# Router logits taken per chunk in five accumulator banks, and expert positions by ten products

## Chip, cores and metric

One NeuronCore of one Trainium2 chip runs the whole program in one launch. The metric is the device time of one execution in microseconds (us). Engines are TensorE (PE for products, PEld for its weight loads), VectorE (DVE), ScalarE (ACT), GpSimd (POOL) and SyncE (SP, which here issues most DMAs).

## What is computed

One step of a two-layer backbone on 640 tokens (128 context, 512 latent; width 1024). The change lies in the second layer's expert network:

```python
def moe_ffn(h, router_w, w_gu, w_down):
    x = h.reshape(B * L, D)
    probs = jax.nn.softmax((x @ router_w).astype(f32), axis=-1)
    top_p, top_i = lax.top_k(probs, TOP_K)                  # 2 of 8
    top_p = top_p / jnp.sum(top_p, axis=-1, keepdims=True)
    gates = jnp.einsum('nk,nke->ne', top_p, jax.nn.one_hot(top_i, N_EXPERTS, dtype=f32))
    for e in range(N_EXPERTS):
        y = y + gates[:, e:e + 1] * swiglu(x, w_gu[e], w_down[e]).astype(f32)
```

`h` is the normed and modulated trunk: `rmsnorm(x, w) * (1 + scale) + shift`.

## The kernel before

The engines run their own instruction lists and meet at semaphores. Activations stand transposed: `hT` holds 8 chunks (`KD`) of 128 features, each 640 tokens wide, that is `NT` = 5 tiles of 128 tokens.

**Accumulators.** `ps` has four slots of 1024 f32 columns, two banks of 512 each. `Ring(4)` deals them out: step j of a stage uses slot j % 4, and `R.plan` counts the uses stage by stage. TensorE calls `take` (wait until the slot's former use is freed), sets `ps_full` with its last product, the reader waits with `full` and frees with `ps_free`; `done` waits for that.

**Weights.** SP loads weight blocks of up to 1 MB into a ring of five places (`load`, L459), in the order of `loads`; a place is loaded again when the step named in the last field of its entry is full. The router's weights (32 KB, 8 chunks of 8 columns) are one such block, "rt". The experts' blocks follow, and need the expert's number first, which DVE writes to `item_expert` (semaphore `items_ready`).

**norm3** (L687 to L730). ACT squares xT, TensorE sums the squares with a matrix of ones (L717), ACT makes `rstd`, DVE writes `hT` chunk by chunk (L728), and ACT adds the shift in place, chunk by chunk (L708), raising `h_ready` by one per chunk: 32 when norm3's last chunk is there.

**Router, TensorE** (`pe_router`). It waits for `h_ready` 32. For each token tile t it sums over the eight chunks k the product of hT's 128 x 128 block (the weights of the array) with the router's 8 columns, 40 products into columns t*8 of one slot. Then 40 transposes turn hT to rows of tokens, eight per tile, each tile in a slot ("ht", L1895). Then the positions ("cnt"): for each tile t, the sum over u < t of `ones` times the one-hot rows of tile u, and the triangle `tri[0]` times those of tile t, so that each token has its rank within its expert; 15 products, and 5 more for the counts.

**Router, DVE** (`dve_router`). It copies the logits (L1912), takes the two largest of each token and their indices (L1915 to L1919), makes the one-hot rows `oh` (L1924 to L1926), the weights (L1928 to L1930), then the low part of each transposed tile, `hlo` (L1934, after ACT's high part `hhi`, L2120). It copies positions and counts (L1937, L1938) and works out the number of items, their experts, and each token's place; `items_ready` comes at L1961, `sel` (L1973, L1976) and `slot_i` (L1968) behind it. POOL adds hhi and hlo to rows (L2178) and scatters these by `slot_i` (L2185).

**Experts.** TensorE gathers the first item's tokens by products with `sel` (`pe_gather`), then runs a loop over items (up to 256 token rows of one expert each), the count and the expert being read from `item_expert` at run time. ACT makes the high part of each weight block (L1996), DVE and POOL the low part (L2002). `rows` of an item are stored and gathered back at the end.

All products go through `mm` (L580). An f32 product shows as two records, each with its load. The other norms use the same helpers; `pe_first`, behind norm2, has a loop with the chunk outermost:

```python
for k in range(KD):
    nc.tensor.wait_ge(h_ready, h_base + k + 1)
    for c in range(chunks_):
        ...
```

Of the kernel before, what the change touches and what calls it, by code (L numbers as in the profile page):

```python
# [29 lines left out]
P = 128  # L30
D = 1024
KD = D // P
# [12 lines left out]
NE = 8  # L45
# [99 lines left out]
def program(nc, I, O):  # L145
    with ExitStack() as ctx:
# [205 lines left out]
        for stage, each, turns in (  # L352
                ("lam", 2, 1), ("mod", 4, MOD_FIRST // 2), ("norm0", 1, 1), ("qkv", 12, 1), ("z", 4, 1), ("gat", 1, 1),
                ("qk", 16, 1), ("l2", 8, 1), ("vb", NT, 1), ("att0", len(plan_b), 1), ("obn", H, 1),
                ("cum", 1, 1), ("tri", len(TRI), 1), ("scan", len(STEP), 1), ("omod", len(OMOD), 1), ("onrm", NT, 1), ("eo", 4, 2),
                ("norm1", 1, 1), ("fgu", 2 * FC, 1), ("fdn", 2, 4),
                ("norm2", 1, 1), ("oi", 7, 1), ("mlan", 2, 1), ("uqn", HC, 1), ("uqr", 8, 1), ("kn", HC, 1),
                ("vv", NT + 1, 1), ("att1", len(plan_c), 1), ("oo", 4, 2),
                ("norm3", 1, 1), ("rt", 1, 1), ("ht", NT, 1), ("cnt", 1, 1), ("moe0", 4, 1),
                ("moe", len(ITEM), ITEMS)):  # L360
            R.plan(stage, each, turns)

# [18 lines left out]
        def take(stage, j, turn=0):  # L381
            s, n, _, free = slot_use(stage, j, turn)
            if not (isinstance(n, int) and n == 0):
                nc.tensor.wait_ge(free[s], n)
            return s

        def full(eng, stage, j, turn=0):
            s, n, written, _ = slot_use(stage, j, turn)
            eng.wait_ge(written[s], n + 1)
            return s  # L390

        def done(eng, stage, j, turn=0):
            s, n, _, free = slot_use(stage, j, turn)
            eng.wait_ge(free[s], n + 1)
# [18 lines left out]
            "kn": (I["w_ukv"][0:1], WB, 1, 1, lambda j: ("kn", HC - 1)),  # L413
            "vv": (I["w_ukv"][1:2], WB, 1, 1, lambda j: ("vv", NT)),
            "oo": (I["w_oo"], WB, 2, 2, lambda j: ("oo", 2 * j + 1)),
            "rt": (I["w_rt"], 64, 1, 1, lambda j: ("rt", 0)),
            "moe": (None, WB, EC + 6, ITEMS, None),
        }
        order = [(stage, j, turn) for stage, (_, _, each, turns, _) in loads.items() if stage != "moe"
# [13 lines left out]
        def block(stage, j, turn=0):  # L433
            s, n = wuse(stage, j, turn)
            nc.tensor.wait_ge(w_full[s], 16 * (n + 1))
            return wring[:, s, :]
# [142 lines left out]
        def mm(out, lhsT, rhs, first, last):  # L579
            return nc.tensor.matmul(out, lhsT, rhs, start=first, stop=last)  # L580
# [1300 lines left out]
        bigf = tmp[:, MISC + 960:MISC + 960 + ITEMS + 1]  # L1881
        whof = tmp[:, MISC + 800:MISC + 800 + ITEMS + 1]

        def pe_router():
            nc.tensor.wait_ge(h_ready, 32)
            w, s = block("rt", 0), take("rt", 0)
            for t in range(NT):
                for k in range(KD):
                    last = mm(ps[:, s, t * NE:(t + 1) * NE], hT[:, k, t * P:(t + 1) * P], w[:, k * NE:(k + 1) * NE],
                              k == 0, k == KD - 1)  # L1890
            last.then_inc(ps_full[s], 1)
            for t in range(NT):
                s = take("ht", t)
                for k in range(KD):
                    last = nc.tensor.transpose(ps[:, s, k * P:(k + 1) * P], hT[:, k, t * P:(t + 1) * P], ident)  # L1895
                last.then_inc(ps_full[s], 1)

            nc.tensor.wait_ge(oh_ready, 1)
            s = take("cnt", 0)
            for t in range(NT):  # L1900
                for u in range(t + 1):
                    mm(ps[:, s, t * NE:(t + 1) * NE], tri[0] if u == t else ones, oh[:, u, :], u == 0, u == t)
            for u in range(NT):
                last = mm(ps[:, s, NT * NE:(NT + 1) * NE], ones, oh[:, u, :], u == 0, u == NT - 1)
            last.then_inc(ps_full[s], 1)

        def dve_router(dve, st):


            dve.wait_ge(mla_out, 32)  # L1910
            s = full(dve, "rt", 0)
            nc.vector.tensor_copy(gates_sb[:, 0:NT * NE], ps[:, s, 0:NT * NE]).then_inc(ps_free[s], 1)  # L1912
            done(dve, "rt", 0)
            for t in range(NT):
                last = nc.vector.max(top[:, t, :], rt[:, t, :])  # L1915
            st.then(last)
            for t in range(NT):
                st.then(nc.vector.max_index(topi[:, t, :], top[:, t, :], rt[:, t, :]))
            nc.vector.tensor_copy(topf, topi)  # L1919
            nc.vector.tensor_tensor(tw, top[:, :, 1], top[:, :, 0], ALU.subtract).then_inc(top_ready, 1)  # L1920
            dve.wait_ge(top_ready, 1)
            for t in range(NT):
                for i, o in enumerate((oh1, oh2)):
                    last = nc.vector.tensor_scalar(o[:, t, :], iota[:, 0:NE], topf[:, t, i:i + 1], None, ALU.is_equal)  # L1924
            st.then(last)
            nc.vector.tensor_tensor(oh, oh1, oh2, ALU.add).then_inc(oh_ready, 1)  # L1926
            dve.wait_ge(top_exp, 1)
            st.then(nc.vector.tensor_scalar(tokw[:, 1, :], tw, 1.0, None, ALU.add))  # L1928
            st.then(nc.vector.reciprocal(tokw[:, 0, :], tokw[:, 1, :]))
            st.then(nc.vector.tensor_tensor(tokw[:, 1, :], tw, tokw[:, 0, :], ALU.mult))  # L1930
            for t in range(NT):
                dve.wait_ge(hhi_ready, t + 1)
                s, _ = R.use("ht", t)
                nc.vector.tensor_tensor(hlo[:, t, :], ps[:, s, :], hhi[:, t, :].bitcast(F32), ALU.subtract  # L1934
                                        ).then_inc(ps_free[s], 1)
            s = full(dve, "cnt", 0)
            nc.vector.tensor_copy(pos, ps[:, s, 0:NT * NE].rearrange("p (t e) -> p t e", e=NE))  # L1937
            nc.vector.tensor_copy(cnt, ps[:, s, NT * NE:(NT + 1) * NE]).then_inc(ps_free[s], 1)  # L1938
            done(dve, "cnt", 0)

            st.then(nc.vector.tensor_scalar(tiles_e, cnt, 0.0, None, ALU.is_gt))
            for m in range(1, -(-T // IT)):
                st.then(nc.vector.scalar_tensor_tensor(tiles_e, cnt, float(m * IT), tiles_e, ALU.is_gt, ALU.add))
            st.then(nc.vector.tensor_tensor_scan(last_e, ones[:, 0:NE], tiles_e, 0.0, ALU.mult, ALU.add))
            nc.vector.tensor_tensor(cmp, spread(last_e, 1, ITEMS + 1), spread(iota[:, 0:ITEMS + 1], 2, NE), ALU.is_le)
            nc.vector.tensor_tensor(started, last_e, tiles_e, ALU.subtract)
            st.then(nc.vector.tensor_tensor(first_e, last_e, tiles_e, ALU.subtract))
            nc.vector.tensor_reduce(whof, cmp, AX.X, ALU.add)
            st.then(nc.vector.tensor_scalar(first_e, first_e, float(IT), -1.0, ALU.mult, ALU.add))
            st.then(nc.vector.tensor_scalar(whof, whof, float(NE - 1), None, ALU.min))  # L1950
            nc.vector.tensor_copy(item_expert[0:1, 0:ITEMS + 1], whof[0:1, :])
            nc.vector.tensor_copy(item_expert[0:1, ITEMS + 1:ITEMS + 2], last_e[0:1, NE - 1:NE])

            st.then(nc.vector.scalar_tensor_tensor(endp, first_e, 1.0, cnt, ALU.add, ALU.add))
            st.then(nc.vector.scalar_tensor_tensor(cmp, spread(iota[:, 0:ITEMS + 1], 2, NE), float(-IT),
                                                   spread(endp, 1, ITEMS + 1), ALU.mult, ALU.add))
            nc.vector.tensor_tensor(begun, spread(iota[:, 0:ITEMS + 1], 2, NE), spread(started, 1, ITEMS + 1), ALU.is_ge)
            st.then(nc.vector.tensor_scalar(cmp, cmp, float(P), None, ALU.is_gt))
            st.then(nc.vector.tensor_tensor(cmp, cmp, begun, ALU.mult))
            st.then(nc.vector.tensor_reduce(bigf, cmp, AX.X, ALU.add))  # L1960
            nc.vector.tensor_copy(item_expert[0:1, ITEMS + 2:2 * ITEMS + 3], bigf[0:1, :]).then_inc(items_ready, 1)  # L1961

            st.then(nc.vector.tensor_tensor(pos, pos, spread(first_e, 1, NT), ALU.add))
            for i, o in enumerate((oh1, oh2)):
                st.then(nc.vector.tensor_tensor(prd, pos, o, ALU.mult))
                st.then(nc.vector.tensor_reduce(slot_of[:, i, :], prd, AX.X, ALU.add))
            dve_select(st)
            nc.vector.tensor_copy(slot_i[:, :, :], slot_of[:, :, :]).then_inc(slot_ready, 1)  # L1968
# [628 lines left out]
```

## Time and profile before

| | us |
|---|---|
| median of 3 runs | 2578.08 |
| lowest, highest | 2575.83, 2585.19 |
| profiled execution, whole time | 2584.36 |
| its span | 2581.9 |
| mean granted TensorE clock of it | 0.926 |

| engine | busy us | share |
|---|---|---|
| PE | 2305.9 | 89% |
| PEld | 2017.9 | 78% |
| DVE | 1057.6 | 41% |
| ACT | 888.7 | 34% |
| POOL | 479.7 | 19% |

Times in the views count from the start of the span. "L580" is line 580 of the kernel; a line can be that of a helper. In a timeline a row is a run of like instructions on one engine, with the idle time before it and what ended that in brackets. "PEclk" is the clock that TensorE was granted, 1.00 being 2.4 GHz and 0.50 being 1.2 GHz.

### The profile page before, as it was taken

The page shows a single profiled execution, that of the slowest core. Times are in us where ns is not written, and L with a number is a line of the kernel's source. Part 1 is how long each engine was busy: PE and PEld are TensorE (multiplying, and loading weights), DVE is VectorE, ACT ScalarE, POOL GpSimd, SP SyncE. Part 2 cuts the span into 40 slices and gives each one's busy share as a digit, 9 for nine tenths or more (in the row PEclk, how much of TensorE's full clock was granted, in tenths as well). Part 3 has the DMA queues.
Part 4 walks back from the last instruction along what each step waited for, and adds up shares of the span by engine and source line. Part 5 has one row for each costly group of instructions (what it writes and reads, how often), then busy time and mean ns, then how long its engine had stood idle before and what let it go on. Part 6 is the DMA issues. An engine that isn't in the chain of part 4 may idle for free.

```text
span 2581.9 us, 35367 instructions
## 1 busy us (share of the span) xinstructions
PE 2305.9 (89%) x14334; PEld 2017.9 (78%) x14335; DVE 1057.6 (41%) x1537; ACT 888.7 (34%) x1259; POOL 479.7 (19%) x266
## 2 busy tenths in 40 slices
PE   6999887848898999989998999969998899998994
PEld 4896665538767999989965587968898888897893
DVE  2521264445723222232113455232335777744534
ACT  3321244212114111131032134124345666644444
POOL 0100002463002000020000000024223454523321
PEclk8989987759999999989999899969999999999997
DMA  6121003940431222211210000017547878866655
GB/s 286 51 90 49 33 25 132 336 176 11 170 114 49 82 69 80 67 45 68 84 56 19 1 33 34 1 49 274 176 172 273 324 307 330 344 227 236 247 190 170
DMA packets 70078, 353.68 MB, mean 137 GB/s; under 512 B 12112, under 2 KB 17872, under 8 KB 37296
## 3 DMA queue, kind: packets, MB, share of 16 engines
q1 hardware_dynamic: 65200, 337.28, 35.5%
q0 software_dynamic: 4736, 14.26, 1.5%
q8 instruction: 119, 1.95, 0.3%
q14 instruction: 23, 0.19, 0.0%
HBM read 318.06 MB, written 33.46 MB: 136 GB/s over the span
## 4 chain that ended last, share of the span: by engine, by line
PE 62%; issue 15%; POOL 9%; DVE 7%; ACT 4%; DMA 3%; SPq 0%; POOLq 0%; DVEq 0%; ACTq 0%
PE ps L580 58%; POOL wring_x L2002 6%; PE ps L717 1%; PE ps L984 1%; ACT arena L1036 1%; POOL tmp L1202 1%; DVE tmp L1487 1%; POOL tmp L1200 1%; POOL arena_x L1689 1%; DVE tmp L1427 1%; DMA xT<-in_x 1%; DVE att L1006 1%; DMA wring<-in_w_mod 1%; POOL rows L2185 0%; ACT hT L708 0%
## 5 line engine op out<-in xcount | busy, mean ns | idle before, releaser
L580 PE MATMUL ps<-arena_x,hT_x 128*128 128x256 f32 (+1 forms) x2536 | 355.8, 293 | 34.3 <-issue 34.3
L580 PE MATMUL ps<-arena_x 128*128 128x320 f32 (+3 forms) x1698 | 361.5, 352 | 17.0 <-DVE arena_x L1976 8.9
L2002 POOL TENSOR_TENSOR wring_x<-wring,arena_x 128x2048 fp32r<-128x2048 f32 (+1 forms) x60 | 284.2, 4745 | 459.1 <-ACT arena_x L1996 459.0
L580 PEld LDWEIGHTS ps<-arena_x,hT_x 128*128 128x128 f32 x2536 | 329.0, 199 | 38.6 <-issue 36.6
L580 PEld LDWEIGHTS ps<-arena_x 128*128 128x128 f32 (+1 forms) x1698 | 279.2, 192 | 65.5 <-issue 31.6
L1996 ACT ACTIVATE arena_x<-wring 128x2048 fp32r<-128x2048 f32 x153 | 284.2, 1857 | 100.4 <-DMA wring<-in_w_mgu 100.4
L2002 DVE TENSOR_TENSOR wring_x<-wring,arena_x 128x2048 fp32r<-128x2048 f32 (+1 forms) x90 | 215.3, 2401 | 81.3 <-ACT arena_x L1996 81.3
L580 PE MATMUL ps<-hT,wring 128*128 128x320 f32 x832 | 233.4, 443 | 12.1 <-ACT hT L708 10.6
L580 PEld LDWEIGHTS ps<-hT,wring 128*128 128x128 f32 x832 | 162.1, 195 | 83.6 <-issue 20.2
L580 PE MATMUL ps<-tmp_x,arena_x 128*128 128x320 f32 x1024 | 165.9, 314 | 6.0 <-ACT hT L708 6.0
L580 PEld LDWEIGHTS ps<-tmp_x,arena_x 128*128 128x128 f32 x1024 | 156.7, 192 | 6.7 <-issue 6.5
L580 PE MATMUL ps<-tmp_x,wring_x 128*128 128x320 f32 x1024 | 161.3, 309 | 0.0
L580 PE MATMUL ps<-wring_x,hT_x 128*128 128x256 f32 x1120 | 153.2, 286 | 8.1 <-POOL wring_x L2002 7.9
L580 PE MATMUL ps<-hT_x,arena_x 128*128 128x320 f32 x960 | 152.8, 310 | 1.2 <-DVE arena_x L1061 0.7
L580 PEld LDWEIGHTS ps<-tmp_x,wring_x 128*128 128x128 f32 x1024 | 152.9, 188 | 0.1
L580 PEld LDWEIGHTS ps<-wring_x,hT_x 128*128 128x128 f32 x1120 | 142.9, 194 | 10.0 <-POOL wring_x L2002 9.1
L580 PEld LDWEIGHTS ps<-hT_x,arena_x 128*128 128x128 f32 x960 | 144.2, 189 | 1.7 <-DVE arena_x L1061 0.9
L2135 ACT ACTIVATE expf<-ps 128x256 f32<-128x256 f32 x110 | 42.2, 384 | 229.0 <-PE ps L580 228.9
L1583 DVE SCALAR_TENSOR_TENSOR xT<-ps,modcol,xT 128x128 f32<-128x128 f32 (+2 forms) x72 | 27.2, 434 | 209.1 <-PE ps L580 209.1
L2225 DVE TENSOR_TENSOR expf<-expf,ps 128x256 f32<-128x256 f32 x110 | 45.4, 415 | 158.7 <-ACT expf L2135 158.7
L1744 DVE TENSOR_TENSOR arena<-arena,ps 128x640 f32<-128x640 f32 x22 | 18.1, 821 | 213.3 <-PE ps L580 213.3
L691 ACT ACTIVATE tmp<-xT 128x640 f32<-128x640 f32 x32 | 22.0, 730 | 180.0 <-DVE xT L1583 154.9
(305 smaller groups left out, 3188.9 us busy)
## 6 DMA issues: line engine op xcount, KB each, us to landing
wring<-in_w_mgu SPq DMA_DIRECT2D x105, 1024.0 KB, 6.0
wring<-in_w_mod SPq DMA_DIRECT2D x48, 1024.0 KB, 9.5
wring<-in_w_mdn SPq DMA_DIRECT2D x30, 1024.0 KB, 5.6
wring<-in_w_gu SPq DMA_DIRECT2D x22, 1024.0 KB, 4.8
wring<-in_w_mdn SPq DMA_DIRECT2D x20, 768.0 KB, 5.2
wring<-in_w_ev SPq DMA_DIRECT2D x14, 1024.0 KB, 5.0
rows<-hT SPq DMA_DIRECT2D x1, 12288.0 KB, 34.5
wring<-in_w_dn SPq DMA_DIRECT2D x16, 704.0 KB, 4.1
```

The source lines that it names most:

```text
L580: return nc.tensor.matmul(out, lhsT, rhs, start=first, stop=last)
L717: last = nc.tensor.matmul(pair(s)[:, half, :], ones, tc[:, k, half * HT:(half + 1) * HT], start=(k == 0), stop=(k == KD - 1))
L984: last = nc.tensor.transpose(ps[:, s, n * P:(n + 1) * P], probs(i, 0)[:, n * P:(n + 1) * P], ident)
L1006: nc.vector.tensor_reduce(cells(i)[:, st_:st_ + 1], src, AX.X if t == 0 else AX.XY, ALU.max, negate=True).then_inc(mx_ready, 1)
L1036: nc.scalar.activation(dst, src, ACT.Exp, bias=cells(i)[:, st_:st_ + 1], accum_out=cells(i)[:, 2 + st_:3 + st_]).then_inc(ps_free[s], 1)
L1200: st.then(eng.tensor_tensor(part, L[:, k + 1:B32, k:k + 1].broadcast_to([NB, rest, n]), X[:, k:k + 1, 0:n].broadcast_to([NB, rest, n]), AL ...
L1202: last = eng.tensor_tensor(X[:, k + 1:B32, 0:n], X[:, k + 1:B32, 0:n], part, ALU.subtract)
L1583: last = nc.vector.scalar_tensor_tensor(xs, ps[:, s, at:at + b - a], modcol[:, bass.ds(c * 2 + (gate * 16 + grp), 1)], xs, ALU.mult, ALU.add)
L1996: nc.scalar.activation(whi[b % 6][:, 0:wsize(b)], wslot[s][:, 0:wsize(b)], ACT.Copy).then_inc(whi_ready, 1)
L2002: eng.tensor_tensor(wslot_x[s][:, 0:size], wslot[s][:, 0:size], whi[b % 6][:, 0:size].bitcast(F32), ALU.subtract).then_inc(ready, 1)
L2135: nc.scalar.activation(sgE[:, j % 2, :, :], pair(s, P), ACT.Silu).then_inc(silu_ready, 1)
L2225: nc.vector.tensor_tensor(actf[:, j % 2, :, :], sgE[:, j % 2, :, :], ps[:, s, :].rearrange("p (m n) -> p m n", m=2)[:, :, P:2 * P], ALU.mu ...
```

## The change

Router logits: the stage "rt" has three accumulator slots in place of one, and each token tile has a bank of its own among their six. The loop over chunks is the outer one and waits for one chunk at a time. The slots are marked full behind tiles 1, 3 and 4 of the last chunk, and DVE copies tile by tile (8 columns each). SP's hold on the router's weight place names the third slot. Positions: one product of `tri[0]` with all 40 one-hot columns, then four of `ones` for the distances 1 to 4 between tiles, of 32, 24, 16 and 8 columns; with the five for the counts, ten.

```diff
-                ("norm3", 1, 1), ("rt", 1, 1), ("ht", NT, 1), ("cnt", 1, 1), ("moe0", 4, 1),
+                ("norm3", 1, 1), ("rt", 3, 1), ("ht", NT, 1), ("cnt", 1, 1), ("moe0", 4, 1),
...
-            "rt": (I["w_rt"], 64, 1, 1, lambda j: ("rt", 0)),
+            "rt": (I["w_rt"], 64, 1, 1, lambda j: ("rt", 2)),
...
+        def logits(s, t):
+
+            return ps[:, s, t % 2 * 512:t % 2 * 512 + NE]
+
         def pe_router():
-            nc.tensor.wait_ge(h_ready, 32)
-            w, s = block("rt", 0), take("rt", 0)
-            for t in range(NT):
-                for k in range(KD):
-                    last = mm(ps[:, s, t * NE:(t + 1) * NE], hT[:, k, t * P:(t + 1) * P], w[:, k * NE:(k + 1) * NE],
+            w, slots = block("rt", 0), [take("rt", i) for i in range(3)]
+            for k in range(KD):
+                nc.tensor.wait_ge(h_ready, 24 + k + 1)
+                for t in range(NT):
+                    last = mm(logits(slots[t // 2], t), hT[:, k, t * P:(t + 1) * P], w[:, k * NE:(k + 1) * NE],
                               k == 0, k == KD - 1)
-            last.then_inc(ps_full[s], 1)
+                    if k == KD - 1 and t in (1, 3, 4):
+                        filled(last, "rt", t // 2)
...
-            for t in range(NT):
-                for u in range(t + 1):
-                    mm(ps[:, s, t * NE:(t + 1) * NE], tri[0] if u == t else ones, oh[:, u, :], u == 0, u == t)
+            ohs = oh.rearrange("p t e -> p (t e)")
+            mm(ps[:, s, 0:NT * NE], tri[0], ohs, True, False)
+            for d in range(1, NT):
+                mm(ps[:, s, d * NE:NT * NE], ones, ohs[:, 0:(NT - d) * NE], False, d == NT - 1)
             for u in range(NT):
                 last = mm(ps[:, s, NT * NE:(NT + 1) * NE], ones, oh[:, u, :], u == 0, u == NT - 1)
...
-            s = full(dve, "rt", 0)
-            nc.vector.tensor_copy(gates_sb[:, 0:NT * NE], ps[:, s, 0:NT * NE]).then_inc(ps_free[s], 1)
-            done(dve, "rt", 0)
+            for t in range(NT):
+                s = full(dve, "rt", t // 2)
+                last = nc.vector.tensor_copy(gates_sb[:, t * NE:(t + 1) * NE], logits(s, t))
+                if t in (1, 3, 4):
+                    freed(last, "rt", t // 2)
+            for i in range(3):
+                done(dve, "rt", i)
```

## Rows read from the trace of the kernel before

**Rows 1.** The page: the chain that ended last, by engine.
```profile
PE 62%; issue 15%; POOL 9%; DVE 7%; ACT 4%; DMA 3%; SPq 0%; POOLq 0%; DVEq 0%; ACTq 0%
```

**Rows 2.** Timeline of norm3: start, length, engine, line, operation, count.
```profile
1673.10 8.77 PE L717 MATMUL ps<-tmp,cst 128*128 128x320 f32 x32
```

**Rows 3.** Chain of waits, 1681 to 1737: start, length, what.
```profile
1685.89 7.44 ACT hT L708 x16
...
1693.37 17.25 PE ps L580 x80
...
1710.71 0.21 DVE gates_sb L1912
...
1715.29 5.76 DVE arena_x L1934 x5
```

**Rows 4.** Windows: from:to, length, busy of each engine, PEclk, DMA share, GB/s.
```profile
1681.87:1686.30 4.43, 0.00 (x1) 0.00 (x0) 1.52 (x4) 3.22 (x5) 0.00 (x0) 0.99 0.00 0
1686.30:1693.37 7.07, 0.00 (x0) 0.00 (x0) 5.97 (x13) 7.02 (x15) 0.00 (x0) 0.50 0.00 0
1693.37:1710.62 17.25, 17.23 (x80) 17.14 (x80) 0.00 (x0) 0.00 (x0) 0.00 (x0) 0.50 0.00 1
1710.97:1716.90 5.93, 5.93 (x28) 5.93 (x29) 5.55 (x33) 2.65 (x4) 0.30 (x1) 0.50 0.00 0
1716.90:1718.30 1.40, 1.40 (x14) 1.30 (x12) 1.40 (x2) 1.22 (x2) 1.40 (x1) 0.99 0.00 0
1721.15:1723.80 2.65, 2.62 (x24) 2.65 (x24) 0.00 (x0) 0.00 (x0) 2.65 (x3) 0.99 0.00 0
1723.80:1727.50 3.70, 3.70 (x18) 3.62 (x17) 0.00 (x0) 0.00 (x0) 3.70 (x2) 0.50 0.00 0
1736.35:1740.90 4.55, 4.52 (x21) 4.55 (x22) 0.01 (x1) 1.91 (x1) 2.73 (x3) 0.51 1.01 405
1740.90:1748.15 7.25, 7.25 (x61) 7.05 (x59) 0.60 (x1) 4.46 (x3) 5.42 (x7) 1.00 1.00 396
```

**Rows 5.** The logits' products: duration in ns, least, median, most.
```profile
L580 PE MATMUL ps<-wring,hT x80: 361/361/383, 1693.4 to 1710.2; 128*128 128x8 f32 x80
```

**Rows 6.** Timeline from the transposes to the first item's products.
```profile
1710.97 7.47 PE L1895 MATMUL ps<-cst,hT 128*128 128x128 f32 x40 [0.36 <-DVE gates_sb L1912]
...
1721.18 6.34 PE L580 MATMUL ps<-tmp,cst 128*128 128x8 f32 x40 [2.74 <-DVE arena_x L1934]
...
1727.56 0.20 DVE L1937 COPY tmp<-ps 128x40 f32<-128x40 f32 x1 [6.52 <-PE ps L580]
...
1733.29 2.59 SPq L459 DMA_DIRECT2D wring<-in_w_mgu  x5
...
1736.38 11.77 PE L580 MATMUL ps<-arena_x 128*128 128x256 f32 x80 [8.86 <-DVE arena_x L1976]
...
1754.60 5.54 PE L580 MATMUL ps<-arena_x,hT_x 128*128 128x256 f32 x32 [6.45 <-issue]
```

**Rows 7.** Timeline behind norm2, where the loop has the chunk outermost.
```profile
1304.76 7.43 ACT L708 ACTIVATE hT<-hT,modcol 128x128 f32<-128x128 f32 x16 [1.14 <-DVE hT L728]
1305.99 0.50 PEld L580 LDWEIGHTS ps<-hT,wring 128*128 128x128 f32 x2 [5.76 <-issue]
...
1306.69 0.34 PEld L580 LDWEIGHTS ps<-hT,wring 128*128 128x128 f32 x1 [0.20 <-issue]
1307.22 0.34 PEld L580 LDWEIGHTS ps<-hT,wring 128*128 128x128 f32 x1 [0.20 <-issue]
```

**Rows 8.** Timeline of SP, 1560 to 1740.
```profile
1574.72 0.42 SPq L459 DMA_DIRECT2D wring<-in_w_rt  x1
```

**Rows 9.** Who waited for whom, 1655 to 1780: us in total, times, longest.
```profile
ACT arena_x L1996 <- DMA wring<-in_w_mgu: 22.2, 3, 18.4
```

**Rows 10.** Chain of waits, 1728 to 1775.
```profile
1728.20 9.37 issue
1737.57 1.05 POOL rows L2185
```

## The prediction

> **What bounds the kernel now.** I began with the page's chain that ended last. TensorE products are 62% of the span [rows 1], so I looked for the stretch that the change touches, the third norm's end to the first expert item, and read it in the timeline, then in the chain of waits there. The reader is to see one string of work without a second branch. The last product of norm3 ends at 1681.87 [rows 2]. ACT then makes the eight shifted chunks of hT from 1685.89 to 1693.33, TensorE starts the logits at 1693.37 and takes 17.25 us for 80 records (two for each of 40 products), and only then DVE copies them [rows 3]. DVE has no gap from there to the end of the five hlo subtractions at 1721.05 [rows 3]. Position counting follows at 1721.18 and DVE's copy of it at 1727.56 [rows 6]. The loads of the first item's weights are issued at 1733.29, the gather starts at 1736.38, the first item's products at 1754.60 [rows 6].
>
> Then I asked the windows what clock each stretch had [rows 4]. TensorE was granted 1.00 until about 1686.3, some 4.4 us after its last product, and 0.50 (the level of 1.2 GHz) from there on, through all 17.25 us of the logits, although it was busy without a gap. It came back to 1.00 in the transposes of hT, and fell again in the middle of the position products. A logits pair (weight load and product) at 0.50 takes 17.25/80 = 0.216 us. In the positions, 24 pairs in 2.65 us at full clock are 0.110 us each.
>
> **Part 1: logits chunk by chunk.** Removed: the wait for the last chunk ahead of product one. Added: eight waits, two more slots taken. The number of products and columns is the same. When can product one start? The second norm has the same pattern, a loop with the chunk outermost: ACT began at 1304.76 and TensorE's first load stood at 1305.99, 1.23 us later [rows 7]. ACT here began at 1685.89, so product one comes at 1687.12, in place of 1693.37: 6.25 us earlier. ACT makes a chunk in 7.44/8 = 0.93 us, TensorE eats one in ten pairs, 2.16 us, so only the first wait can be felt. The clock was already at 0.50 by 1687.12 [rows 4], so I leave the pair at 0.216. The end of the logits moves from 1710.62 to 1704.37, and TensorE sets it, not ACT. The overlap is partial: 6.25 of 7.44 us.
>
> Slots: the first holds norm3's sums, freed when ACT has made rstd, before DVE's first multiply; the other two were freed by the residual additions, ahead of norm3. None is late. The router's weights were issued at 1574.72 [rows 8]. SP's later hold on that ring place asks for the third router slot in place of the first, and is asked only behind the item's number, long after.
>
> The five banks and the changed order could cost something that no row shows directly. From below nothing, at most a few per cent gained; from above the recorded times without overlap, 0.361 us a product [rows 5], +11.6 us in all. The nearest row is the second norm's: product loop across four slots with waits between, at 0.50, where loads stand 0.53 us apart (1306.69, 1307.22) [rows 7], which is the streaming of 320 columns with the loads hidden beneath. So I take 0.
>
> **Part 2: the copy.** One copy of 40 columns (0.21 us [rows 3]) becomes five of eight. Four run while TensorE is still busy: two tokens before the first flag, two before the second. Behind the last product stands one copy. Its fixed part is nearly all of the 0.21, so gain 0.05, and two more checks on the queue eat it: 0. Were all five exposed, it would be about 0.8 us more. Queued behind it are the top-k steps, as before. The transposes now need not wait for the copy (they began 0.35 us after the logits [rows 3, 6]), but DVE reaches the first hlo only 4.6 us after its copy [rows 3], so that is hidden. ACT's halves for it follow the transposes, and they too come the same amount earlier.
>
> **Part 3: positions.** Twenty products (40 pairs, 6.34 us [rows 6]) become ten (20 pairs). Products of 8 to 40 columns replace those of 8: norm3's 320 columns take 8.77/32 = 0.274 us [rows 2], so 40 take 0.034, less than the load's 0.110. Only the count matters. All at full clock 20 × 0.110 = 2.2 us, all at half 20 × 0.216 = 4.3 us. Before, the clock fell 2.65 us into them [rows 4], about 5.5 us after the transposes; after the last norm product it fell after 4.4, so it isn't certain that all 20 fit. I take 2.9, a third of the way from full to half, since the fall is as likely behind them as in them: a gain of 3.45 with ends 2.0 and 4.1. All of it lies on the path: DVE waited for the result.
>
> **Sum.** 6.25 + 0 + 3.45 = 9.7 us, 0.38%. Is it kept? Everything from DVE's copy at 1727.56 on hangs on that copy: the item's number, SP's loads, slot_of and with it the POOL scatter, the selection matrices, the gather. ACT waits for the first weights (22.2 us in three waits [rows 9]), and these loads start when the number is there, so the transfers move too. POOL's hrow sums hang on hlo, which moves 6.25, and were done 9.37 us before the scatter [rows 10]; with 3.45 less they still are. I see no event with a date of its own. The price of all moved work is therefore 0. The profiled execution took 2584.36 us (span 2581.9 and 2.46 around it); less 9.7 it is 2574.7. It was a long one, 6.3 above the median of the runs, so the forecast is set from the median: 2578.08 − 9.7 = 2568.4.
>
> **A rule against the row.** The windows show 0.50 over 80 dense pairs of 8 columns [rows 4], and a fall inside a dense row of such pairs. The Trainium skill, TensorE: Matmul & The Clock Gate, Part 1, has it that sustained activity releases the clock. Its Part 4 says that the full clock does not engage for transposes; by that the positions would start at half, 4.3 us, and the whole gain would be 8.3. The trace does not agree: the clock came back during them [rows 4].
>
> **Rivals.**
> A, *the clock returns in the logits.* In the gather the clock came back 4.55 us after its start [rows 4]. If the earlier, unbroken start let the logits do so, 4.55 us would be 21 pairs at 0.216, the other 59 take 0.110: 11.0 us, end at 1698.2, 12.4 earlier; with 3.45 it is 15.9: **2562.2**. For it: the idle stretch shrinks from 11.5 to 5.25 us, so the fall may come just after the restart. Against it: the same pairs held 0.50 for 17 us, and could not hold 1.00 in the positions. By the page's rule on sustained activity this would be the outcome; the trace does not agree. Chance 0.09.
> B, *the clock takes part of it back.* The positions run at half speed throughout (gain 2.0), and the clock returns 3 us later in the gather and in the first item. In the gather 21 records took 4.55 us at 0.50 (0.217 each) and 61 took 7.25 at 1.00 (0.119) [rows 4], so each us later costs 0.45: 2.7 in the two. That leaves 6.25 + 2.0 − 2.7 = 5.55: **2572.5**. For it: these stretches are all short. Against it: the clock is as likely to come earlier. Chance 0.08.
> C, *the pair is no longer overlapped* (the other side). If a change of bank or a wait ahead of it keeps the next load from running under the product, a pair costs its 0.361 us [rows 5]: 28.9 us, end at 1716.0, 5.4 later than before; less 3.45 it is 1.95 slower: **2580.0**. It decides from (17.25 + 6.25 + 3.45)/80 = 0.337 us a pair. Against it: the second norm. Chance 0.06, and half of that takes in something worse that I have not seen.
>
> **How the numbers follow.** A measurement of this kernel tells about 0.5% (12.9 us) from no change. The forecast's case has 0.77, by itself 2566.2 to 2569.8 (2.0 to 4.1 for the positions, up to 1.5 more where the clock falls only after the logits have begun). The three runs before span 9.4 us, so a median can be 2 or 3 off; one in eight of that case then passes 2565.2. With A that is faster 0.18; slower 0.03 out of C; the rest same, 0.79. The range takes in A's edge and B's: 2562.5 to 2574.5.
>
> **What would show it.** First load of the logits 1.2 us after ACT's first shifted chunk; 80 pairs in 17.2 us at 0.50; DVE's last copy some 0.1 us behind them; top-k steps and five hlo subtractions as long as before; 20 position pairs in 2.3 to 4.4 us; the first weight load at about 1723.6 on the old time axis; gather and first item that much earlier. Wrong if pairs stand over 0.25 us apart, if a hlo waits on ACT, if the weight loads don't move with the number, or if the later items show more idle time for TensorE than before.

## The result, and the profile after

The changed kernel takes 2549.49 us (median of 4 runs, 2546.59 to 2553.25) against 2576.95 us before (4 runs, 2575.39 to 2585.19): a ratio of **0.9869, 95% interval 0.9848 to 0.9890**. The forecast was 2568.4 with a range down to 2562.5. The sign was right and the size was not: nearly three times as much was gained, and most of it in a stage that the change doesn't touch.

The profiled execution of the changed kernel has a span of 2546.8 us, 35.1 shorter. Some 4.5 us of that lie ahead of norm3, where nothing differs: norm3's first product stands at 1668.57 in place of 1673.10, and in the fourteen profiles of this study it lies between 1668.57 and 1677.25. So I count from it in what follows.

First the stretch of the prediction. Timeline of the changed kernel (start, length, engine, line, operation):

```profile
1668.57 8.78 PE L717 MATMUL ps<-tmp,cst 128*128 128x320 f32 x32
...
1681.37 7.43 ACT L708 ACTIVATE hT<-hT,modcol 128x128 f32<-128x128 f32 x16 [1.14 <-DVE hT L728]
...
1682.52 17.20 PE L580 MATMUL ps<-wring,hT 128*128 128x8 f32 x80 [5.18 <-ACT hT L708]
...
1699.76 0.17 DVE L1919 COPY gates_sb<-ps 128x8 f32<-128x8 f32 x1 [0.19 <-PE ps L580]
...
1704.41 5.75 DVE L1944 TENSOR_TENSOR arena_x<-ps,arena_x 128x1024 fp32r<-128x1024 f32 x5
1705.72 9.27 POOL L2188 TENSOR_TENSOR tmp<-arena_x 128x1024 f32<-128x1024 f32 x4 [330.85 <-DVE arena_x L1944]
...
1710.30 2.54 PE L580 MATMUL ps<-tmp,cst 128*128 128x40 f32 x20 [3.26 <-DVE arena_x L1944]
1712.88 0.20 DVE L1947 COPY tmp<-ps 128x40 f32<-128x40 f32 x1 [2.72 <-PE ps L580]
1712.99 0.16 DVE L1948 COPY tmp<-ps 128x8 f32<-128x8 f32 x1
1713.18 1.84 DVE L1951 TENSOR_SCALAR tmp<-tmp 128x8 f32<-128x8 f32 x1
1714.96 2.33 POOL L2188 TENSOR_TENSOR arena<-arena_x 128x1024 f32<-128x1024 f32 x1
1715.06 2.46 DVE L1953 SCALAR_TENSOR_TENSOR tmp<-tmp 128x8 f32<-128x8 f32 x2
...
1722.19 2.61 SPq L459 DMA_DIRECT2D wring<-in_w_mgu  x5
...
1725.28 11.65 PE L580 MATMUL ps<-arena_x 128*128 128x256 f32 x80 [12.44 <-DVE arena_x L1986]
...
1741.46 6.29 PE L580 MATMUL ps<-arena_x,hT_x 128*128 128x256 f32 x32 [4.53 <-issue]
```

| us from norm3's first product | before [rows 2, 3, 6] | after | gained so far |
|---|---|---|---|
| first logits product | 20.27 | 13.95 | 6.32 |
| first position product | 48.08 | 41.73 | 6.35 |
| DVE's copy of the positions | 54.46 | 44.31 | 10.15 |
| gather | 63.28 | 56.71 | 6.57 |
| first item's products | 81.50 | 72.89 | 8.61 |
| end of the span | 908.8 | 878.2 | 30.6 |

The reader sees three things. Up to the copy of the positions the gain is 10.15 us where 9.7 had been forecast. Then 3.6 us of it go, in two small DVE operations: L1951 takes 1.84 us and L1953 2.46 for two. They end where POOL's sums end (1714.99 and 1717.29); in the kernel before they took 0.35 and 0.37 us. The kernel before:

```profile
1725.85 2.33 POOL L2178 TENSOR_TENSOR arena<-arena_x 128x1024 f32<-128x1024 f32 x1
...
1727.87 0.35 DVE L1941 TENSOR_SCALAR tmp<-tmp 128x8 f32<-128x8 f32 x1
1728.25 0.37 DVE L1943 SCALAR_TENSOR_TENSOR tmp<-tmp 128x8 f32<-128x8 f32 x2
```

The first item gets 2.0 us of it back, since the idle stretch ahead of it is 4.53 us in place of 6.45. Last, 22 us come behind the first item, where not a line was changed.

The clock of TensorE in this stretch, from the windows of the changed kernel (as rows 4):

```profile
1677.35:1682.50 5.15, 0.00 (x0) 0.01 (x1) 2.24 (x6) 3.95 (x6) 0.00 (x0) 0.92 0.00 0
1682.52:1699.72 17.20, 17.20 (x81) 17.20 (x82) 5.70 (x15) 6.28 (x14) 0.00 (x0) 0.50 0.00 1
1710.30:1712.84 2.54, 2.54 (x20) 2.44 (x20) 0.00 (x0) 0.00 (x0) 2.54 (x3) 0.91 0.00 0
```

The logits held the 1.2 GHz level throughout although they began after only 5.15 us of idle time, so rival A did not occur.

Where do the 22 us come from? The timelines of TensorE show it, at the items' first products. Kernel before, from 1830 to 2425 (the number in brackets is the idle time ahead, and "issue" says that the profile shows nothing that was waited for):

```profile
1859.99 5.72 PE L580 MATMUL ps<-arena_x,hT_x 128*128 128x256 f32 x32 [5.42 <-issue]
...
1965.82 3.77 PE L580 MATMUL ps<-arena_x,hT_x 128*128 128x256 f32 x16 [5.68 <-issue]
...
2026.10 3.77 PE L580 MATMUL ps<-arena_x,hT_x 128*128 128x256 f32 x16 [5.46 <-issue]
...
2359.40 3.78 PE L580 MATMUL ps<-arena_x,hT_x 128*128 128x256 f32 x16 [5.89 <-issue]
```

The fifth stands at 2420.73, with 5.45 us. The same view of the changed kernel, where these are all over 1 us:

```profile
1843.43 4.09 PE L580 MATMUL ps<-arena_x,hT_x 128*128 128x256 f32 x32 [1.25 <-issue]
...
2000.48 3.78 PE L580 MATMUL ps<-arena_x,hT_x 128*128 128x256 f32 x16 [5.45 <-issue]
...
2384.95 5.52 PE L580 MATMUL ps<-arena_x,hT_x 128*128 128x256 f32 x32 [3.59 <-issue]
```

Five idle stretches of 27.9 us became three of 10.3. Most of the remaining 4.4 of the 22 us is the slow start behind such a stretch: the first 32 records of the second item took 5.72 us behind 5.42 idle us, and 4.09 behind 1.25. The granted clock in the first 1.61 us of it, before and after:

```profile
1859.99:1861.60 1.61, 1.61 (x7) 1.61 (x8) 0.00 (x0) 0.00 (x0) 0.00 (x0) 0.50 0.43 148
1843.43:1845.04 1.61, 1.61 (x13) 1.61 (x14) 1.61 (x2) 0.00 (x0) 0.00 (x0) 1.00 0.75 239
```

Items 3 and 9 start 1.7 us faster in the same way, and the first item 0.75 us slower (6.29 against 5.54 us). The five stretches stand at the loop's turn from item 1 to 2, 2 to 3, 3 to 4, 8 to 9 and 9 to 10. Items 1, 2, 8 and 10 are big (256 rows), so four of the five turns lead from or to a big item, and 3 to 4 joins two small ones. At the turns from 4 to 8 there is none. And the page's DMA queue of instructions, before:

```profile
q8 instruction: 119, 1.95, 0.3%
```

and after:

```profile
q8 instruction: 101, 1.65, 0.3%
```

Eighteen fewer packets, of 1.95/119 = 0.0164 MB each. In the 17 us around the second item's start it is four packets before and one after. The trace also holds TensorE's branch instructions. Before, the branch back at the end of item 1 stands at 1854.27, a packet starts at 1854.97 and takes 1.21 us, and the loop's first test comes at 1857.82. After, branch and test stand at 1841.54 and 1842.05, with no packet between them.

**Theory 1.** TensorE's program is read in such pieces, and the item loop is too long to be held whole. Whether its head and tail must be read again when it turns depends on where the loop stands. The change takes ten f32 products out (four instructions each: two loads, two products) and puts one wait in: the loop stands 39 instructions earlier. The trace has 18980 TensorE instructions ahead of the loop's first test before the change and 18941 after it, which is the 39. A big item has 698 product records and a small one 357, each with its load, so the loop has some 2260 instructions with the waits (estimate). The Trainium skill, Runtime: NRT & Kernel Launch, section Instruction fetch mechanics, says that TensorE buffers 2048 instructions, refilled in blocks of 256 (16 KiB), and that a taken branch whose target is not in the current window of two such blocks (it calls them pages) waits for a fetch. The packet size above agrees with the skill's 16 KiB; the 2048 no run here shows by itself. With the window of two blocks the trace does not agree: the loop's head lies some 2260 instructions back, nearly nine blocks, and yet the turns from item 4 to 8 take 0.5 us from branch to test, with no packet.

**Theory 2.** The items start at another time against the weight transfers, and fall into a better rhythm. **Theory 3.** The accumulator slots or the wait by chunk act on later stages. A fourth question apart: did DVE wait for POOL?

### The profile page after: what moved, and what is told of

Read it like the earlier page. It is cut to its first block, busy times and chain, and to the rows that moved or that the text cites. A ratio compares the mean times of both kernels' runs of the same rounds, so it can differ in the third digit from the quotient of the medians.

```text
span 2546.8 us, 35323 instructions
## 1 busy us (share of the span) xinstructions
PE 2291.7 (90%) x14314; PEld 2005.9 (79%) x14315; DVE 1061.6 (42%) x1541; ACT 888.9 (35%) x1259; POOL 480.2 (19%) x266
## 4 chain that ended last, share of the span: by engine, by line
PE 63%; issue 14%; POOL 9%; DVE 7%; ACT 4%; DMA 3%; SPq 0%; POOLq 0%; DVEq 0%; ACTq 0%
PE ps L580 59%; POOL wring_x L2012 6%; PE ps L717 1%; PE ps L984 1%; ACT arena L1036 1%; POOL tmp L1200 1%; POOL tmp L1202 1%; POOL arena_x L1689 1%; DMA xT<-in_x 1%; DVE tmp L1487 1%; DVE tmp L1427 1%; DMA wring<-in_w_mod 1%; DVE att L1006 1%; POOL rows L2195 0%; DVE arena L1020 0%
## 5 line engine op out<-in xcount | busy, mean ns | idle before, releaser
L580 PE MATMUL ps<-arena_x,hT_x 128*128 128x256 f32 (+1 forms) x2536 | 350.1, 290 | 14.8 <-issue 14.8
L580 PEld LDWEIGHTS ps<-arena_x,hT_x 128*128 128x128 f32 x2536 | 323.9, 196 | 18.8 <-issue 16.3
```

## The experiments

Each kernel was compared with the kernel before on the same chip. "Place" is the number of TensorE instructions by which the item loop stands later than before, as the traces count them, blocks of 256 left out; "items" the time from the first item's first product to the end of the span in its one profile; "stalls" the idle stretches over 2.5 us at the head of an item.

| kernel | place | ratio to before (95%) | median us | packets | items us | stalls |
|---|---|---|---|---|---|---|
| before | 0 | 1 | 2576.95; 2582.58, 2583.58 and 2583.51 in the later sets | 119 | 827.3 | 5 |
| after | −39 | 0.9869 (0.9848–0.9890) | 2549.49 | 101 | 805.3 | 2 |
| logits only | +1 | 0.9964 (0.9942–0.9986) | 2574.9 | 120 | 822.4 | 5 |
| positions only | −40 | 0.9915 (0.9891–0.9938) | 2559.62 | 101 | 805.4 | 2 |
| after, 39 more | 0 | 0.9953 (0.9932–0.9975) | 2569.43 | 120 | 824.2 | 5 |
| before, 217 more | −39 | 0.9904 (0.9883–0.9926) | 2559.97 | 103 | 804.1 | 2 |
| after, sums moved | −39 | 0.9865 (0.9831–0.9900) | 2549.93 | 101 | 802.6 | 2 |
| after, 20 more | −19 | 0.9880 (0.9840–0.9919) | 2553.9 | 102 | 804.8 | 2 |
| after, 128 more | +89 | 0.9951 (0.9934–0.9968) | 2571.58 | 120 | 821.0 | 3 |
| after, 217 more | −78 | 0.9852 (0.9812–0.9891) | 2546.71 | 101 | 795.4 | 0 |
| the same, split otherwise | −78 | 0.9864 (0.9843–0.9885) | 2548.33 | 101 | 801.7 | 0 |
| the same, sums moved | −78 | 0.9846 (0.9825–0.9867) | 2543.62 | 101 | 800.8 | 0 |
| after, 195 more | −100 | 0.9852 (0.9826–0.9878) | 2544.6 | 101 | 796.1 | 0 |
| before, no branch hint | −1 | 1.0005 (0.9988–1.0022) | 2583.55 | 121 | 825.2 | 4 |

**Logits only.** The changed kernel with the old positions:

```diff
-            ohs = oh.rearrange("p t e -> p (t e)")
-            mm(ps[:, s, 0:NT * NE], tri[0], ohs, True, False)
-            for d in range(1, NT):
-                mm(ps[:, s, d * NE:NT * NE], ones, ohs[:, 0:(NT - d) * NE], False, d == NT - 1)
+            for t in range(NT):
+                for u in range(t + 1):
+                    mm(ps[:, s, t * NE:(t + 1) * NE], tri[0] if u == t else ones, oh[:, u, :], u == 0, u == t)
```

> The change's logits part with the old twenty position products; the loop over items stands one TensorE instruction later than before. Theory 1 (place of the code: the item loop is short of 39 instructions ahead of it, and the instruction fetches at its back edge fall away): the items run as before, 827 us from the first item's product to the end of the span, idle stretches of 5.4 to 5.9 us between items stay, instruction queue near 119 packets; only 6.3 us are gained, about 2570. Theory 2 (the items gain because they start at another time against the weight transfers): a good part of the 22 us comes with a start that is 6 us earlier, 2550 to 2560. Theory 3 (the five accumulator slots or the wait by chunk do something to later stages): the whole 22 us come, about 2548.

Measured: 0.9964, that is 9 us by the ratio (4 to 15 by its interval), 120 packets, and the stretches back. Its timeline at item 2 and 3:

```profile
1857.65 6.15 PE L580 MATMUL ps<-arena_x,hT_x 128*128 128x256 f32 x32 [5.46 <-issue]
...
1964.00 3.78 PE L580 MATMUL ps<-arena_x,hT_x 128*128 128x256 f32 x16 [5.78 <-issue]
```

The logits began 13.95 us behind norm3's first product, as in the changed kernel, so the whole of the forecast's part 1 was there, and the 22 us were not. Theory 3 falls. (With the new logits ten of the loop's semaphore instructions, one per item, are register operations, with the same count in all; that is so here too, and gave nothing.) Against theory 2: the items began 5.1 us earlier and gained 5, of which 3.9 are shorter stretches at items 4 and 10 (3.50 and 3.54 us). The clock fell before the positions here (0.50 in all of them), and these took 8.67 us for the same 40 records that took 6.34 before.

**Positions only.** The kernel before with the four lines removed above in place of its own.

> The ten position products with the old logits; the loop over items stands 40 instructions earlier. Theory 1: the items gain 20 us as in the changed kernel, the idle stretches at items two and three go, the instruction queue shows near 101 packets, about 2554 to 2558 in all. Theory 2: a part of it only, since the start is some 0 to 4 us earlier. Theory 3: 2573 to 2577. Beside that: DVE's two small operations behind the position copy meet POOL's sums, whose end moves by nothing, while the copy comes 3.8 us earlier; by the theory that DVE waits there for POOL they take some 3.5 us more than before, and the local gain is near nothing.

Measured: 0.9915 (22 us), 101 packets, items in 805.4 us, and the local gain gone as foreseen: the positions took 2.37 us, then DVE's timeline read

```profile
1719.65 0.20 DVE L1938 COPY tmp<-ps 128x40 f32<-128x40 f32 x1 [2.55 <-PE ps L580]
1719.77 0.16 DVE L1939 COPY tmp<-ps 128x8 f32<-128x8 f32 x1
1719.96 2.02 DVE L1942 TENSOR_SCALAR tmp<-tmp 128x8 f32<-128x8 f32 x1
1721.92 2.33 POOL L2179 TENSOR_TENSOR arena<-arena_x 128x1024 f32<-128x1024 f32 x1
1722.01 2.46 DVE L1944 SCALAR_TENSOR_TENSOR tmp<-tmp 128x8 f32<-128x8 f32 x2
```

and the gather began 63.10 us behind norm3, against 63.28 before. The items began only 1.9 us earlier than before and gained 21.9, which theory 2 can't give. So part 3 saves nearly nothing where it stands, and 22 us through the place of the loop.

**After, 39 more.** The waits ask for a level long reached; two in the source make one instruction.

```diff
+            for _ in range(78):
+                nc.tensor.wait_ge(consts_in, 16)
```

> The changed kernel, with 39 instructions that only look at a semaphore long set, on TensorE behind the position products, where it waits 12 us for the selection matrices anyway; so the item loop stands where it stood before. Theory 1: the 20 us are lost again, the idle stretches of 5.4 us at items two and three come back, instruction queue near 119 packets, about 2568. Theories 2 and 3: no change against the changed kernel, 2549.

Measured: 0.9953 against 0.9869, 120 packets, items in 824.2 us. Nothing of the change was undone, and yet most of its gain went. Its first product of item 2:

```profile
1848.93 5.89 PE L580 MATMUL ps<-arena_x,hT_x 128*128 128x256 f32 x32 [5.50 <-issue]
```

**Before, 217 more.** The same two lines in the kernel before, with 220 at the head of `pe_router` and 214 behind the position products.

> The kernel before, with 217 such instructions on TensorE in two stretches where it is idle (ahead of the logits and behind the positions); 217 more is the same as 39 fewer where blocks of 256 instructions (the 16 KB of one packet of the instruction queue) are counted. Nothing else differs from before. Theory 1: the items gain some 20 us, 2555 to 2560, instruction queue near 101 packets plus one. Theories 2 and 3: 2577 or a few us more.

Measured: 0.9904 (25 us), 103 packets, items in 804.1 us, with TensorE's item 2 at

```profile
1857.91 4.09 PE L580 MATMUL ps<-arena_x,hT_x 128*128 128x256 f32 x32 [1.18 <-issue]
```

A kernel that does all the work of before and 217 idle instructions more is 1% faster. This run and the last show that the place sets the time. That it acts through the reading of instructions is shown by the loop's turns: the fourteen traces of this study have 154 of them. In 37 a packet of the instruction queue starts between the branch back and the loop's first test, and these take 3.2 to 7.7 us. The other 117 have none, and take 0.4 to 0.7 us. Six turns of eleven have one in the kernel before (the last of them behind item 10), two in the changed kernel.

**After, 20, 128, 217 and 195 more.** The same lines with other numbers (128 all behind the positions; 110 of the 217 and 75 of the 195 ahead of the logits).

> The changed kernel with 20 instructions that only look at a set semaphore ahead of the item loop: halfway between its place and the one of before. Theory 1 has no finer forecast than that the time depends on the place alone: it lies near the changed kernel (some 101 packets of the instruction queue, 2550) or near the kernel with 39 (some 120 packets, 2569) if whole blocks decide, in between only if single instructions count.

> 128 of them, half a block. The loop's code is some 2260 instructions, 8.8 blocks of 256, so it touches nine blocks from few places and ten from most. By theory 1 this is one of the many: some 115 to 125 packets, 2565 to 2572. If the time hung on the exact distance alone, without a block structure, nothing would be foretold.

> 217 of them, in two idle stretches of TensorE: 39 fewer than a block, so 78 earlier than the kernel before where blocks are counted. By the count of blocks a place 39 further down is either still among the good ones (101 to 103 packets, 2550) or over the edge (115 to 125 packets, 2568).

> The changed kernel with 195 such instructions: 22 places beyond that with 217, 100 earlier than the kernel before. Measured from the first item to the end so far: 822 to 827 us at 0 and +1, 821 at +89, 805 at -40, -39 and -19, 795 at -78. Theory 1 has it on one of these levels, with the packets of the instruction queue going with it; a time between levels would speak against it.

Measured: places −19 and −40 belong together, 0, +1 and +89 do, and between them lies a step: 20 instructions cost nothing, 39 cost 20 us. The packets go with it, 101 to 103 on one side, 119 to 121 on the other. At one and the same place the stretches at items 4 and 10 still differ between profiles by up to 2 us. There the packet starts only 2.1 to 5.0 us behind the branch, at the other stalled turns within 0.9; why, no run shows. What I had not foreseen is a further step at −78 and −100: there the stretches at items 4 and 10 are gone too, with as few packets (101), and only the turn to item 2 shows anything:

```profile
1853.19 4.09 PE L580 MATMUL ps<-arena_x,hT_x 128*128 128x256 f32 x32 [1.24 <-issue]
```

It is worth little: 795.4 to 801.7 us for the items against 802.6 to 805.4, and the intervals of the whole kernels overlap. The count that I gave beforehand (nine blocks from few places, ten from most) doesn't fit as it stood, since the five places tried between −100 and −19 are all good, and that is a stretch of 82 of 256. Which part of the loop is held from where stays open.

**After, the POOL sums moved.**

```diff
             for t in range(NT):
+                if t == 3:
+                    pool.wait_ge(slot_ready, 1)
                 done(pool, "ht", t)
```

> The changed kernel, but POOL makes only its first three hrow sums when they can be had, and the last two after DVE's slot numbers are there (ahead of the scatter). The number of TensorE instructions stays. If DVE's operations behind the position copy waited for POOL's sums (1.84 us, and 2.46 for two, where before they took 0.35 and 0.37), they fall to some 0.2 and 0.4, and the gather starts 3.7 us earlier after the position copy; the scatter and POOL's first low part of a weight block then end about where they did, so 1 to 3 us are left at the end. The rival, that these two operations are long by themselves or wait for something of TensorE's: they stay at 1.8 and 2.5, and the time rises a little through the later scatter.

Measured, DVE's and POOL's timeline:

```profile
1712.00 6.97 POOL L2190 TENSOR_TENSOR tmp<-arena_x 128x1024 f32<-128x1024 f32 x3 [331.00 <-DVE arena_x L1944]
1716.59 4.41 PE L580 MATMUL ps<-tmp,cst 128*128 128x40 f32 x20 [3.52 <-DVE arena_x L1944]
...
1721.34 0.17 DVE L1951 TENSOR_SCALAR tmp<-tmp 128x8 f32<-128x8 f32 x1
1721.54 0.37 DVE L1953 SCALAR_TENSOR_TENSOR tmp<-tmp 128x8 f32<-128x8 f32 x2
...
1729.73 2.37 POOL L2190 TENSOR_TENSOR tmp<-arena_x 128x1024 f32<-128x1024 f32 x1 [10.75 <-DVE att L1978]
```

From DVE's copy of the positions to the gather it is 8.64 us in place of 12.40. So DVE did wait for POOL: the two operations fell from 1.84 to 0.17 and from 2.46 to 0.37. The Trainium skill, SBUF — State Buffer, section Who interferes with whom, has the rule: a DVE instruction with two SBUF inputs contends with a GpSimd one that reads SBUF, and so does one in a two-port mode, where whoever issues first has the shared ports for its whole instruction. The trace agrees for L1953, which has two SBUF inputs: it was held to the end of POOL's instruction of 2.33 us. The copies L1947 and L1948, which read the accumulator, ran beside POOL's sum in 0.20 and 0.16 us. L1951 has one SBUF input and was held too; whether it ran in a two-port mode no trace shows. Of the whole kernel's time the 3.8 us left no trace (0.9865 against 0.9869), and the first item began 72.37 us behind norm3 against 72.89. In this profile the clock fell before the positions (4.41 us in place of 2.54), and POOL's first low part of a weight block began at 1749.27, 74.4 us behind norm3 against 71.95.

**217 more, twice again.** Both with 78 ahead of the logits and 139 behind the positions; one of them with the sums moved. The logits aren't held up (13.95 us behind norm3 in both), but the gather is: the 139 instructions reach to about 1728.7 in the first run, and the gather starts 13.0 us behind the copy of the positions, where the changed kernel has 12.40.

> The same 217 instructions, with the sums as in the changed kernel. Theory 1 says that the place alone sets the time of the items: 795 us from the first item's product to the end again (the changed kernel 805), first item 73 us behind norm3, 2542 to 2547. If the 795 us were chance in the single profile of the earlier run, it shows 803 to 806.

> The changed kernel with 217 instructions that only look at a set semaphore (78 ahead of the logits, 139 behind the position products, so that TensorE is idle there anyway; in the run with 110 ahead they took 0.064 us each and the logits began 1.9 us late), and POOL's last two sums behind the slot numbers. From the first item's product to the end 795 us as in the run with 217, and the first item 72.4 us behind the start of norm3 as in the run with the moved sums: 2540 to 2545, the fastest so far. If the two gains are one and the same, it is no faster than 2547.

Measured: 2548.33 and 2543.62. The 795 us did not come again: 801.7 and 800.8, which neither branch of my expectation had (795, or 803 to 806), while the run with 195 more shows 796.1. So the kernels without a stretch spread over 6 us, and why stays open. With the sums moved the two DVE operations took 0.17 and 0.37 us again, but the gather came 11.34 us behind the copy of the positions in place of 8.64, since TensorE was still busy with the idle instructions; my expectation's "so that TensorE is idle there anyway" did not hold. The 2543.62 lies in the 2540 to 2545 that I expected, but by luck: neither the 795 us nor the first item at 72.4 us came (73.97). The ratio of 0.9846 is the lowest of the study, but its interval reaches over that of the changed kernel: between the four fastest kernels I can't say which is best. They beat the kernel before by 1.4 to 1.5%.

**Before, no branch hint.**

```diff
-            with nc.Fori(0, ITEMS, engines=(mybir.EngineType.PE,), hint_back_edge=True) as i:
+            with nc.Fori(0, ITEMS, engines=(mybir.EngineType.PE,)) as i:
```

> The kernel before without the instruction at the head of TensorE's item loop that hints at the branch back; the loop stands in the same place but for that one instruction. If the idle stretches between items are fetches of the code that the branch back goes to, there are more of them now: idle of some 5 us also at small items, where before TensorE went on within 1.5 us, and 10 to 30 us more in all. If they come from the register reads and waits at the head of an item, nothing changes: 2577 to 2583.

Measured: 1.0005, 121 packets. My expectation missed. The stretches grew a little and moved (6.15 at item 2, 6.17 at item 3, 6.43 at item 9, and 5.23 at item 5, a small item that had none), while those at items 4 and 10 went:

```profile
q8 instruction: 121, 1.98, 0.3%
```

At a stalled turn two packets now start between the branch back and the first test, one after the other, and the turns to items 2, 3 and 9 and the last take 5.0 to 5.1 us each, where they take 3.2 to 3.6 before. But five turns stall in place of six, and the time is the same. This kernel's loop also stands one instruction earlier and is one shorter, and no run has that with the hint in place: so which turns stall can't be put down to the hint alone. The alternative that I had written down, that nothing would change, holds for the time and not for the stretches.

## Why the prediction was right and wrong

**Part 1, right.** 6.25 us forecast, 6.32 measured. The start forecast 1.2 us behind ACT's first chunk was 1.15; the pair stayed at 17.20/80 = 0.215 us at half clock; no bank or wait made it longer, so rival C is refuted.

**Part 2, right.** The last copy began 0.04 us behind the last product, and DVE reached hlo 4.65 us after it, with no gap in the five subtractions (5.75 us).

**Part 3, right in its price and wrong in its worth.** The positions took 2.54 us where I took 2.9, between the ends 2.2 and 4.3. The ten profiles with the same ten products show 2.37 to 2.54 in six and 4.13 to 4.41 in four, and nothing near the 2.9 between: the clock's spread was right, its middle stands for no case. But the sentence "All of it lies on the path: DVE waited for the result" failed: DVE waited for the result, and then for POOL. I had written that POOL's sums move by 6.25 us, and asked only whether they would be done in time for the scatter, not what stood beside them on DVE. Before, the position copy came at 1727.56 and POOL's last sum ended at 1728.2 [rows 6, 10], so it was there to be seen that 3.45 us less would slide DVE's next operations under it. Price: 3.6 us, nearly all of the 3.8 that part 3 gained. The first weight load came at 1726.7 on the old time axis (1722.19 + 4.53), where I had named 1723.6. That the first item still began 8.6 us earlier, near the 9.7, is in part luck: 1.9 us of it are the shorter idle stretch ahead of it, which stood in no term of the sum.

**The step that failed** is the last of the sum: "I see no event with a date of its own. The price of all moved work is therefore 0." What moved was not only work in time but code in place. The change removes 40 instructions of TensorE and adds one, ahead of a loop that is too long to be held, and 18 of 119 packets of the instruction queue and 17.6 us of idle time at the head of items fell away; with the slow starts it was 22 us. Shown by addition and by removal: 39 idle instructions take most of the gain away (0.9953), 217 give it to the kernel before (0.9904). The chain of waits gave 15% of the span to "issue" before the change [rows 1]. I did not ask what it was, nor what stood in the 6.45 us ahead of the first item [rows 6]. My last sign of being wrong did look at the later items' idle time, but only for more of it.

The parts add up within their intervals: logits only 0.9964 times positions only 0.9915 is 0.9880, against 0.9869. The range of 2562.5 to 2574.5 would have held the kernel at the old place (2569.43), and for the kernel as it is it was narrower than what I knew of its code. It also stopped 0.3 us short of rival A's own 2562.2.

**The rivals.** A and C did not occur, and B not in the measured profile. Its first half, positions at half speed throughout, stands in four of the ten profiles with the new products, and so was likelier than its 0.08; the 3 us later clock in the gather is in none (the 80 records took 11.4 to 12.5 us, against 11.77 before). The true rival, a term of 20 us for the place of the loop, was not on the list.

## What to carry to other kernels

When a kernel ends in a loop with a long body, count what a change adds or removes in that engine's program ahead of it: the packets of the instruction queue and the idle stretches marked "issue" at the head of an iteration tell whether the place of the code counts, and some dozens of idle instructions can try other places, put where the engine waits anyway and few enough to fit into the wait. A change whose gain appears in a stage that it doesn't touch should be run once more with its code length restored before it is believed. When work on DVE is moved earlier, look at what POOL has running there, not only at what the moved work waits for.

## What the runs showed of the hardware

- The place of a loop of some 2260 TensorE instructions, all else equal, moves the time by 20 us of 2577: 20 instructions ahead of it cost nothing, 39 cost the 20 us, and 217 ahead of the loop of the kernel before gain them. A turn of the loop takes 3.2 to 7.7 us from the branch to the first test where a packet of the instruction queue starts in it, and 0.4 to 0.7 where none does.
- Instructions that only look at a reached semaphore stand 0.108 to 0.110 us apart in TensorE's list (means of their rows in five runs). The 110 ahead of the logits began at 1681.04, which is 5.0 us before norm3's last product ended, and reached to about 1692.7; the logits started at 1693.11, 1.91 us late. The 0.064 us in one of my expectations came from dividing the idle 7.08 us by 110, as if they began with it, and is wrong. Where 75 or 78 stand there, the logits are not late.
- A POOL sum of 128 x 1024 held a DVE operation of 8 columns for nearly its whole 2.33 us (2.29 in the run with 20 more); without it this takes 0.17 us.
- The 80 records of 8 columns (the logits) ran without a gap for 17.2 us at a granted clock of 0.50 throughout, whether 11.5 or 5.2 us of idle time stood before them.
